# RWKV chain of a hybrid decoder: the chunk's output products go to the other half of the PSUM partitions, beside the state's sum

## The reference, cut to what matters

```python
def _wkv_step(S, inp):
    r, k, v, w, kk, b = inp
    sa = jnp.einsum('bhij,bhj->bhi', S, -kk)
    S = S * w[:, :, None, :] + sa[..., None] * b[:, :, None, :] + v[..., None] * k[:, :, None, :]
    return S, jnp.einsum('bhij,bhj->bhi', S, r)
...
    S_T, o = lax.scan(_wkv_step, S0.astype(f32), xs)
```

## Time and profile before

| what | value |
|---|---|
| three runs | 3622.28, 3629.0, 3632.74 us, median 3629.0 |
| the profiled execution's own time | 3623.95 us |
| its span | 3622.1 us |
| PE busy / weight loads busy | 96% / 91% of the span |
| VectorE / ScalarE / GpSimd busy | 51% / 39% / 12% |
| matmul records | 40925, of which some 7900 in each RWKV stage |
| mean granted TensorE clock | 0.985 of full speed |

### The profile page before, as it was taken

How to read it: one execution, slowest core, us unless ns; L and a number is a source line. 1 busy time by engine, 2 the same in 40 slices (tenths; PEclk the granted TensorE clock), 3 DMA queues, 4 the chain that set the end, 5 groups by cost and what they waited for, 6 DMA issues and landing times.

```text
span 3622.1 us, 95147 instructions
## 1 busy us (share of the span) xinstructions
PE 3494.9 (96%) x40925; PEld 3296.5 (91%) x40925; DVE 1857.9 (51%) x2829; ACT 1400.1 (39%) x2392; POOL 426.0 (12%) x570
## 2 busy tenths in 40 slices
PE   7989999999999999899999999999899899999999
PEld 6988879999999855699999999999899787799999
DVE  7545545555356644365533446553374555455532
ACT  4545533443222533344432224442244454244421
POOL 0023230111000000011100101110000332211100
PEclk9999999999999999999999999999999999899999
DMA  3210002222222387422222222222222000122222
GB/s 122 92 39 5 4 26 93 81 82 88 87 82 84 116 301 298 179 84 81 81 90 88 86 81 87 81 82 89 91 76 88 10 4 27 40 87 84 81 90 85
DMA packets 97091, 314.72 MB, mean 87 GB/s; under 512 B 19074, under 2 KB 20354, under 8 KB 96018
## 3 DMA queue, kind: packets, MB, share of 16 engines
q1 hardware_dynamic: 88706, 288.79, 23.8%
q10 hardware_dynamic: 8080, 21.34, 1.6%
HBM read 297.30 MB, written 12.79 MB: 86 GB/s over the span
## 4 chain that ended last, share of the span: by engine, by line
PE 93%; DVE 3%; ACT 2%; issue 1%; DMA 0%; POOL 0%; SPq 0%; ACTq 0%; DVEq 0%
PE ps L418 24%; PE ps L416 23%; PE ps L417 23%; PE ps L1459 6%; PE ps L1017 1%; PE ps L1538 1%; PE ps L2034 1%; PE ps L1635 1%; PE ps L2069 1%; PE ps L2089 1%; PE ps L1128 1%; PE ps L2133 1%; PE ps L1532 1%; PE ps L1033 1%; PE ps L1138 1%
## 5 line engine op out<-in xcount | busy, mean ns | idle before, releaser
L416 PE MATMUL ps<-xh,wh 128*128 128x288 f32 x4656 | 1385.8, 298 | 3.0 <-DVE xl L2419 1.9
L418 PE MATMUL ps<-xh,wl 128*128 128x288 f32 x4656 | 1381.5, 297 | 0.0
L417 PE MATMUL ps<-xl,wh 128*128 128x288 f32 x4656 | 1358.7, 292 | 0.0
L391 ACT ACTIVATE wh<-raw 128x1024 fp32r<-128x1024 f32 x415 | 440.2, 1061 | 1244.0 <-PE ps L418 1205.6
L417 PEld LDWEIGHTS ps<-xl,wh 128*128 128x128 f32 x4656 | 888.8, 191 | 1.6 <-issue 0.5
L416 PEld LDWEIGHTS ps<-xh,wh 128*128 128x128 f32 x4656 | 875.9, 188 | 7.4 <-issue 3.5
L418 PEld LDWEIGHTS ps<-xh,wl 128*128 128x128 f32 x4656 | 873.6, 188 | 0.0
L398 DVE TENSOR_TENSOR wl<-raw,wh 128x1024 fp32r<-128x1024 f32 x415 | 508.5, 1225 | 520.1 <-ACT wh L391 514.3
L418 PE MATMUL ps<-hh,wl 128*128 128x288 f32 x1536 | 457.4, 298 | 0.0
L417 PE MATMUL ps<-hl,wh 128*128 128x288 f32 x1536 | 455.2, 296 | 0.0
L416 PE MATMUL ps<-hh,wh 128*128 128x288 f32 x1536 | 453.9, 295 | 0.0
(11 more groups left out here) (357 smaller groups left out, 4868.1 us busy)
## 6 DMA issues: line engine op xcount, KB each, us to landing
raw<-in_w SPq DMA_DIRECT2D x415, 512.0 KB, 3.5
kp<-in_cache_k SPq DMA_DIRECT2D x64, 512.0 KB, 5.7
vp<-in_cache_v SPq DMA_DIRECT2D x64, 512.0 KB, 6.0
rkv<-in_wkv ACTq DMA_DIRECT2D x2, 2048.0 KB, 9.4
out_wkvs<-rkv ACTq DMA_DIRECT2D x2, 2048.0 KB, 7.2
out_k<-qk ACTq DMA_DIRECT2D x1, 2304.0 KB, 7.0
out_v<-vg ACTq DMA_DIRECT2D x1, 2304.0 KB, 12.1
out_x<-x SPq DMA_DIRECT2D x8, 288.0 KB, 4.7
```

The source lines that it names most:

```text
L391: act.activation(wh[:, c % SPL], raw[:, c % RAWS], ACT.Copy).then_inc(s_hi, 1)
L416: pe.matmul(out, w_h, rhs_h, start=(first and k == 0), stop=False)
L417: pe.matmul(out, w_h, rhs_l, start=False, stop=False)
L418: mm = pe.matmul(out, w_l, rhs_h, start=False, stop=(last and k == nk - 1))
```

## The change

The three output products of a chunk all stand in part 2 now, and each goes crosswise: with the operands of head r it writes the PSUM partitions of the other head, in the same bank 4. Each follows a product of the state's sum with the same head's operands: L1550 (now L1545) with the product of the old state, L1551 (now L1548) with that of the values, L1553 (now L1551) with that of u. The output of a tile thus lies in PSUM with its two heads exchanged, and two ScalarE copies of 64 partitions each (L1572) turn it back, where one of 128 partitions stood (L1574). The wait for the tile's previous copy (`a_oe`) moves with the first output product from part 1 of chunk 0 to part 2.

```diff
--- before.py
+++ after.py
@@ -1537,24 +1537,21 @@
                 for r in HEADS:
                     mm = pe.matmul(u_[r], sl["m5"][r, g], xb[r], start=True, stop=True)
                 mm.then_inc(a_cu, 1)
+            if part == 2:
+                after(pe, a_ue, n)
                 if g == 0:
                     after(pe, a_oe, B.cnt(1, 1))
-                for r in HEADS:
-                    if g:
-                        pe.matmul(out[r], was[r], B.ar[r, g, 1], start=True, stop=False)
-                    pe.matmul(out[r], sl["vst"][r, g], sl["ark"][r, g], start=(g == 0), stop=False)
-            if part == 2:
-                after(pe, a_ue, n)
-                for r in HEADS:
-                    if g:
-                        pe.matmul(s_[r], mview("ist")[r], was[r], start=True, stop=False)
+                for r, cross in zip(HEADS, HEADS[::-1]) if g else ():
+                    pe.matmul(s_[r], mview("ist")[r], was[r], start=True, stop=False)
+                    pe.matmul(out[cross], was[r], B.ar[r, g, 1], start=True, stop=False)
+                for r, cross in zip(HEADS, HEADS[::-1]):
                     pe.matmul(s_[r], sl["ktok"][r, g], sl["vst"][r, g], start=(g == 0), stop=False)
-                for r in HEADS:
-                    mm = pe.matmul(s_[r], sl["btok"][r, g], ust[r], start=False, stop=True)
-                mm.then_inc(a_cs2, 1)
-                for r in HEADS:
-                    mm = pe.matmul(out[r], ust[r], sl["arb"][r, g], start=False, stop=True)
-                mm.then_inc(a_co, 1)
+                    pe.matmul(out[cross], sl["vst"][r, g], sl["ark"][r, g], start=(g == 0), stop=False)
+                for r, cross in zip(HEADS, HEADS[::-1]):
+                    ms = pe.matmul(s_[r], sl["btok"][r, g], ust[r], start=False, stop=True)
+                    mo = pe.matmul(out[cross], ust[r], sl["arb"][r, g], start=False, stop=True)
+                ms.then_inc(a_cs2, 1)
+                mo.then_inc(a_co, 1)
 
         def chain_act(act, B, g, part):
             sl, n = slots[B.s], B.tile(NCK, g + 1)
@@ -1571,8 +1568,9 @@
                     .then_inc(a_s, 1)
                 if g == NCK - 1:
                     act.wait_ge(a_co, n)
-                    act.activation(B.row(rkv, 0), bank(4).rearrange("p (c t) -> p c t", t=CT), ACT.Copy)\
-                        .then_inc(a_oe, 1)
+                    for r, cross in zip(HEADS, HEADS[::-1]):
+                        op = act.activation(B.row(rkv, 0)[r], bank(4)[cross].rearrange("p (c t) -> p c t", t=CT), ACT.Copy)
+                    op.then_inc(a_oe, 1)
 
         def no_chain(eng, B, g, part):
             pass
```

## The result

The changed kernel is slower: 3637.05 us median of 20 runs (3625.85 to 3645.16) against 3628.34 for the kernel before on the same chip (20 runs, 3621.58 to 3632.74). The ratio is 1.0023, with a 95% interval of 1.0016 to 1.0031. The forecast of 3608, with a range to 3631, had the wrong sign. The profiled execution has a span of 3631.6 us, against 3622.1.

What follows compares the result with a forecast made beforehand. PE's way through the two RWKV stages, a loop of latencies in each chunk, was taken as the bound. 17.4 + 5.6 - 2 = 21 us less gave about 3603 profiled, 3608 median, range 3588 to 3631.

Steps and rivals of the forecast that it cites:

- Part 1: Output products leaving part 1 let the sum start sooner where PE came after the copy of u: 17.4 us gained.
- 0.21 less: Sign to look for in the profile after: chunks 6 and 7 each about 0.21 us shorter.
- Part 2, the sum beside the outputs: Crosswise products between the sum's products in part 2 run at once with them and delay its last by 0.
- The tail without L1556: Output product gone from the end of part 2, L1532 sooner in chunks 2, 3 and 7: 5.6 us gained.
- The slower rival: Sum queues behind the outputs in part 2, up to 0.35 us later each: 24 us more, 3653, chance 0.09.
- The second copy: Added ScalarE copy at a tile's end delays L1292 and L1234: 2 us lost, bounds 0 to 6.7.
- The clock: Granted clock 0.98 in a stage: some 5 us at its lower level; a shifted stretch may move 3 us either way.
- rival 2: Other waits or an instruction-arrival limit on PE take part 1's gain: only 4 us less, 3625, chance 0.23.
- issue time that grows by what is gained: Sign of a wrong prediction: PE's stops put to "issue" lengthen by as much as the change gains.
- the forecast's own gain of 23: Gains from output products leaving part 1, 17.4 us, and the tail of part 2, 5.6 us, before the copy's cost.
- The first half of rival 2: With 0.23 us less PE work between half rounds, an inversion step waiting on ScalarE or VectorE copies replaces the chain's wait.
- copies end few of the waits: Evidence against other waits taking the gain: VectorE and ScalarE end only 4.7 of 52.7 us idle before L1459's loads.

Runs made afterwards that it cites:

- e4: The changed kernel without the output products of chunks 1 to 6 (576 matmuls less): 3604.74 us, 0.9943 of the kernel before.
- e1: The kernel before, products straight, with a tile's output copied by two ScalarE instructions of 64 partitions: 3627.52 us, 1.0007 of the kernel before.
- e2: The changed kernel with one ScalarE copy of 128 partitions, heads left exchanged: 3628.75 us, 1.0010 of the kernel before.
- e12: Against the kernel before: outputs crosswise, two of three left in part 1, one copy, heads left exchanged: 3620.40 us, ratio 0.9991.
- e13: The changed kernel with a burst of 1024 products ahead of each RWKV stage's first sum, half of them crosswise in the first stage: 3749.56 us, ratio 1.0338.
- e3: Against the kernel before: outputs crosswise, two of three left in part 1, one beside the sum, two copies: 3621.85 us, 0.9988; again 0.9992.

## Why the prediction was wrong

**Part 1.** Right in where PE came too late, and the lateness went as forecast. The sum is bound to the copy of u in 77 chunks, before in 24. What it is worth in time was never measured by itself; e4, with the same early start and fewer instructions, is 20.6 us faster, and that it is near 21 is in part luck, because e4 has less work as well. Nor did all chunks become shorter where it was forecast. By the distance from one copy of x to the next, chunks 4 and 5 are 0.23 and 0.12 us shorter on the mean, but chunk 6 is 0.26 longer (3.18 to 3.44) and chunk 7 is 0.66 longer (5.54 to 6.20), where 0.21 less was forecast for each. In these two PE's waits for issue grew most, by 6.5 and 6.7 us over all tiles.

**Part 2, the sum beside the outputs.** Right: 0 was taken and 0.03 us measured, 74 bound chunks of it 2.2 us. The tail without L1556 gave about what was counted in chunks 2 and 3, where L1532 comes 0.14 and 0.11 us sooner after the copy of the state; at chunk 7 nothing of it is seen. The slower rival had asked for 0.26 and more. It did not happen; the kernel is slower by another way.

**The second copy.** 2 us forecast, inside the bounds of 0 to 6.7. e1 says 2.4 in the stages, e2 by the ratios 1.8 to 4.7, and e12 none. The way was in part another: the forecast looked at L1292 and L1234, and PE is seen to wait for the copy at L1033, 3.2 us in five times.

**The clock.** The prediction read 0.98 as some 5 us at the lower level in a stage. The trace has 10.2 us of the first stage at the lower of its two levels (1.2 and 2.4 GHz), half of which is what 0.98 costs. Only the 3 us for the clock in the range hung on it.

**The step that failed** is the one on rival 2: "Were they a limit on how fast instructions arrive, denser matmuls would only lengthen them." It was written down, and then given 0.23 and priced as no more than the loss of part 1's gain, 3625. The sum itself put it at nothing. The runs put 25.0 us in its place: PE's issue waits in the two stages went from 19.2 to 44.2. That is one of the prediction's own signs of being wrong, issue time that grows by what is gained. With the forecast's own gain of 23, the sum is -23 + 25.0 + 2.4 for the copy + 2.2 for the interleaving = +6.6, and the stages became 8.1 us longer. This is a tally and not a measurement, since the 23 is the forecast's. In the windows themselves PE is busy for 34.0 us less, waits 25.0 us longer for issue and 8.8 us longer for other engines. The first half of rival 2, that other waits take the chain's place, is thus a smaller part of the truth.

Two things point at it in hindsight. The stage issues 7884 matmuls and as many loads in 263 us, 62 blocks of 256, one in 4.3 us; the DMA view of that window counts 63 transfers of instructions. A burst that takes all it can get (e13, not known then) had one in 3.64. The stage stood at 85% of the supply on the mean, which leaves little room for a stretch at twice the density. And the earlier trace rows had 46.3 us of "issue" which the prediction left unexplained. That "copies end few of the waits" was taken as evidence against the rival; it rather spoke for it, since something else then had to end the waits.

That e3 loses less to it than the changed kernel fits this, as far as the counts go: it puts two crosswise products into part 1 and leaves less of a burst in part 2, and its issue waits grew by 13.6 and not 25.0. No step between the two was measured.

## What to carry to other kernels

Many small matmuls can have a third limit beside the array and the latencies: the rate at which their instructions arrive. Divide the records of a stage, loads included, by 256 and compare the time of a block with what a long row of them needs. Where a stage stands near it, as here at 85%, running products side by side bought nothing, and fewer instructions did (e4). Spreading the dense stretches out lost less than packing them (e3, 0.9988 against 1.0023).

Idle time with the releaser "issue" should be taken for a limit of its own until something else is shown. Look in the DMA view at what is transferred just before such a stop ends, and price the answer in the sum.

Read the mean granted clock of all runs before a difference of a few us is explained.

## What the runs showed of the hardware

- PE's instructions come in 16 KB blocks, one in 3.64 us on the mean of a burst that takes all it can, 28 ns a record of a 64x64 f32 product with its load. PE goes on 2.3 to 2.8 us after the start of a block's transfer in all 16 stops of that burst, and 2.3 to 3.0 us after it in 49 of the 63 stops of the changed kernel's stages.
- Two crosswise and two straight products of the same pair of heads start within 0.02 us, and 24 records took 0.36 us, but a burst of 2048 took 58.2 us, as many straight ones 60.5.
- A 64x64 product with 16 columns instead of 64 leads to the next almost as late, 0.09 to 0.11 us for four records against 0.12.
- The kernel before, with half a block of instructions more, was 6.3 us faster, with a granted clock of 0.9862 against 0.9845 and unchanged issue waits.
